# State space mixer: one 128x512 product of constants in place of two ahead of each diagonal product

## The reference, cut to what matters

```python
cum = jnp.cumsum(dtc * A.astype(f32).reshape(G, R), axis=2)
seg = jnp.exp(jnp.where(lower, cum[:, :, :, None] - cum[:, :, None, :], -jnp.inf))
cb = jnp.einsum('bnigs,bnjgs->bnijg', Cc, Bc)
y_diag = jnp.einsum('bnijg,bnijgr,bnjgrp->bnigrp', cb, seg, dtc[..., None] * xc)
```

## Time and profile before

| What | Value |
|---|---|
| Median of 3 runs | 2821.26 us (2821.2 to 2822.55) |
| The profiled execution's own time | 2822.18 us |
| Its span in the profile | 2820.0 us |
| Mean granted PE clock over the span | 0.984 |
| The mixers' stretch | about 350 to 627 us from the span's start |
| PE busy over the whole span | 2663.9 us (94%) |
| DVE, ACT and POOL busy | 1275.2, 519.9 and 585.0 us |

### The profile page before, as it was taken

The page is one execution under the profiler, slowest core; times in us unless marked ns, Lnnn a source line. Parts: engine busy times, 40 slices in busy tenths (PEclk is TensorE's granted clock), DMA queues, the critical chain, the costliest instruction groups (busy, mean ns, idle before and its releaser), DMA issues. The chain is left out here.

```text
span 2820.0 us, 45984 instructions
## 1 busy us (share of the span) xinstructions
PE 2663.9 (94%) x20286; PEld 2003.0 (71%) x20286; DVE 1275.2 (45%) x1976; ACT 519.9 (18%) x1032; POOL 585.0 (21%) x328
## 2 busy tenths in 40 slices
PE   6999889989999999999888899999999999999998
PEld 4655577764888887444676648888878754788886
DVE  1213234442899954222677544452242373544333
ACT  3222122221111101112444210000010162100001
POOL 0000055520000000001222104443334200334442
PEclk9999999999999999999999999999999999999999
DMA  6123100002222123111000011222222200222220
GB/s 288 71 109 149 60 2 2 2 28 103 80 90 90 64 82 124 45 67 54 33 3 3 3 60 60 90 90 90 90 91 90 90 1 30 89 78 79 85 90 31
DMA packets 17222, 196.33 MB, mean 70 GB/s; under 512 B 1880, under 2 KB 2008, under 8 KB 5248
## 3 DMA queue, kind: packets, MB, share of 16 engines
q1 hardware_dynamic: 17024, 193.39, 18.1%
HBM read 191.27 MB, written 2.12 MB: 69 GB/s over the span
## 5 line engine op out<-in xcount | busy, mean ns | idle before, releaser
L3217 PE MATMUL psum<-arena,weight_ring 128*128 128x256 f32 x3072 | 672.9, 381 | 2.8 <-ACT arena L3107 2.8
L3217 PEld LDWEIGHTS psum<-arena,weight_ring 128*128 128x128 f32 x3072 | 585.3, 191 | 84.9 <-ACT arena L3107 5.3
L1816 PE MATMUL psum<-arena,weight_ring 128*128 128x256 f32 x1584 | 348.2, 381 | 5.0 <-DVE arena L1992 4.0
L1816 PEld LDWEIGHTS psum<-arena,weight_ring 128*128 128x128 f32 x1584 | 302.4, 191 | 47.9 <-issue 6.4
L483 PE MATMUL psum<-arena,weight_ring 128*128 128x512 f32 (+1 forms) x672 | 248.1, 529 | 5.4 <-ACT arena L626 2.7
L2345 POOL TENSOR_TENSOR arena<-arena,consts_sb 128x512 f32<-128x512 f32 x48 | 64.6, 1353 | 902.4 <-ACT arena L2694 692.8
L483 PEld LDWEIGHTS psum<-arena,weight_ring 128*128 128x128 f32 x672 | 127.9, 193 | 117.1 <-issue 105.6
L3316 POOL TENSOR_TENSOR weight_ring<-arena,weight_ring 128x1024 f32<-128x1024 f32 x32 | 79.3, 2478 | 379.8 <-PE psum L3217 379.8
L3306 POOL TENSOR_TENSOR arena<-weight_ring 128x1024 f32<-128x1024 f32 x32 | 77.0, 2405 | 303.8 <-POOLq L3000 274.3
L226 PE MATMUL psum<-arena,weight_ring 128*128 128x512 f32 x320 | 137.8, 593 | 0.0
L3339 ACT ACTIVATE arena<-psum 128x512 f32<-128x512 f32 (+1 forms) x24 | 12.6, 524 | 622.6 <-PE psum L3217 622.6
(11 more groups left out here) (472 smaller groups left out, 3842.1 us busy)
## 6 DMA issues: line engine op xcount, KB each, us to landing
weight_ring<-in_mlp_up SPq DMA_DIRECT2D x16, 2048.0 KB, 7.8
weight_ring<-in_mlp_down SPq DMA_DIRECT2D x16, 2048.0 KB, 7.8
weight_ring<-in_ada SPq DMA_DIRECT2D x12, 2048.0 KB, 12.0
weight_ring<-in_gate_up SPq DMA_DIRECT2D x11, 2048.0 KB, 7.7
weight_ring<-in_w_in SPq DMA_DIRECT2D x7, 2048.0 KB, 10.9
weight_ring<-in_w_o SPq DMA_DIRECT2D x4, 2048.0 KB, 7.8
weight_ring<-in_w_kv SPq DMA_DIRECT2D x4, 2048.0 KB, 8.0
weight_ring<-in_down_a SPq DMA_DIRECT2D x4, 1536.0 KB, 6.5
```

The lines of the kernel that those rows point to most:

```text
L1816: mm = pe.matmul(g.banks[i][:, pair * half:(pair + 1) * half], left[:, j, pair * P:(pair + 1) * P], right(j), start=first and j == 0, stop ...
L3217: mm = pe.matmul(g.banks[i][:, pair * HALF:(pair + 1) * HALF], left[:, j, pair * P:(pair + 1) * P], right(j), start=first and j == 0, stop ...
```

## The change

One of the two products of constants ahead of each `ydiag` product is removed. Nothing else changes; all later lines of the file move up by one, so L1213 of before is L1212 of the changed kernel.

```diff
                     elif kind == "ydiag":
-                        for _ in range(2):
-                            keep_busy(pe, g, bank, SEQ)
+                        keep_busy(pe, g, bank, SEQ)
                         pe.wait_ge(s.m4, 2 * m + d + 1)
                         pe.wait_ge(s.dtx, 2 * m + d + 1)
```

## The result

| | Before | After |
|---|---|---|
| Median | 2821.23 us | 2833.94 us |
| Lowest and highest | 2818.39 to 2824.24 (6 runs) | 2826.0 to 2836.33 (6 runs) |
| Ratio to before, 95% interval | | 1.0038, 1.0022 to 1.0054 |
| Profiled execution, its span | 2822.18, 2820.0 us | 2836.33, 2834.1 us |

The change makes the kernel slower by 0.38%, some 11 us by the ratio. The forecast was 2821.4 us with a range up to 2826.0, and a chance of 0.06 for slower by over 0.2%. It forecast no change; the loss is clear of noise, and the median lies above the range.

The account below looks back on a forecast made before the run. PE was taken to bound the kernel, busy for 2663.9 of 2820.0 us. Profiled 2822.18 - 2.92 gained at d1 uses + 3.06 for two clock falls = 2822.3 us, as a median 2821.4 us; range 2817.5 to 2826.0 us.

Parts of the forecast that it names:

- the gain: At the four d1 uses PE is late, so removing a product there saves 2.92 us in sum; d0 uses gain zero.
- The 0.1 us that the forecast took back at m0 and m2: At m0 and m2 d1, the released L1213 group takes 2.00 instead of 1.90 us, reducing the gain by 0.1 us each.
- The rival in which all eight gain 6.88 us: L1440 moves up at d0 uses too, so all eight uses gain: 2814.4 us; chance 0.03.
- break even below two of them: Gain over price of a clock fall, 2.92 / 1.53 = 1.9 falls; from the second on the change doesn't pay.
- two falls, 3.06 us: Two new clock falls behind the longer PE waits at m1 and m3 d0, costing 3.06 us.
- A fall costs what the groups in it take longer: 1.53 us: Price of one clock fall in the mixers: L1109 0.82 us longer and L1205 0.71 us longer.
- six falls, 9.18 us: Upper bound of the clock term: a fall at every d0 use and two more at groups that shift, 9.18 us.
- the lengths of waits before the two falls of before: Mixer waits of 1.39 and 1.46 us preceded falls; m1 and m3 d0, at 1.57 and 2.15 us, exceed both.
- its rival on the slower side: Clock falls at all four d0 uses and once or twice elsewhere: four falls 2824.5 us, six 2827.5 us; chance 0.18.
- the program runs at PE's pace: Whole kernel: PE is busy for 2663.9 of 2820.0 us and so bounds it.

Follow-up runs that it names:

- d0_one: Kernel before with one product of constants instead of two at the four d0 uses, two kept at d1 uses; median 2829.6 us, ratio to before 1.0025.
- m3_d0_one: Kernel before with one product of constants less at m3 d0 alone; median 2823.65 us, ratio to before 1.0002.
- c_after: The changed kernel run again without any edit, as a control; ratio to before 1.0027, stretch 157.4 us.
- one_each_side: Kernel before with its two products of constants kept at each use, the second moved behind the waits for L1440 and dtx; ratio to before 1.0008.
- m1_d0_one: Kernel before with one product of constants less at m1 d0 alone; ratio to before 1.0019, profiled execution 2821.11 us.
- d1_one: Kernel before with one product of constants instead of two at the four d1 uses, two kept at d0 uses; median 2818.3 us, ratio to before 0.999.
- the kernel with three and one: Kernel before with three products of constants at d0 uses and one at d1 uses, run twice; medians 2818.02 and 2818.03 us, ratios 0.998 and 0.9992.

## Why the prediction was wrong

**Right: the gain.** The forecast gave 2.92 us at the d1 uses and nothing at the d0 uses. With the clock kept up, by the third product at d0 uses, the stretch is 3.0 us shorter in two profiles, split over the four uses as worked out (0.8, 0.9, 0.6 and 0.9 us by the steps, less 0.1 for the third product). The 0.1 us that the forecast took back at m0 and m2, for a longer group, doesn't show in the steps (0.8 and 0.6 where it had 0.71 and 0.49). The rival in which all eight gain 6.88 us has nothing for it, and the waits at d0 uses in the changed kernel (1.30, 1.72, 1.35 and 2.14 us) are close to the forecast's 1.30, 1.57, 1.35 and 2.15.

**Right: the mechanism, and that it could turn the sign.** Falls of the clock at the d0 uses were named as the place, with break even below two of them. Their number lay inside the forecast's one to three: both profiles of the changed kernel have three new ones, at m0, m1 and m3 d0, where the point took two, at m1 and m3.

**Wrong: the size of the term "two falls, 3.06 us".** The step that failed is "A fall costs what the groups in it take longer: 1.53 us". It took one fall of before, which was over after two groups, as the price of every fall. But a fall costs by how long the clock then stays down. In the earlier trace rows that was 3.4 us (from 384.72 to 388.13); behind m3 d0 it held for four groups, 10.2 us, and behind m1 d0 in one execution for 30.7 us. With the gain put back, the stretch lost 147.4 - 141.5 + 3.0 = 8.9 us in the first profile of the changed kernel, and 157.4 - 141.5 + 3.0 = 18.9 us in the second, where 3.06 were forecast. With the 0.8 us at m0 d0 ahead of the stretch that is 3.2 and 6.6 us for each of the three falls, in place of 1.53.

Measured in time at the lower level the price is steadier: 8.9 us for 21.9 us more of it, 18.9 for 45.9, in `d0_one` 7.9 for 19.6 and in `m3_d0_one` 4.4 for 10.2. That is 0.40 to 0.43 us for each microsecond, and the forecast's own 1.53 for 3.4 us is 0.45. So the price per microsecond was right and the microseconds were not. The Trainium skill (TensorE: Matmul & The Clock Gate, Terms) gives 0.5 as the penalty at half clock; the trace is somewhat below it, perhaps since PE waits for others in part of that time. Even the upper bound of the forecast (six falls, 9.18 us) was no bound: it just holds the first profile's loss, not the second's.

The unprofiled runs bear this out. Over the twelve runs of `c_after` the mean clock is 0.9799 against 0.9847, some 27 us more at the lower level in each. At 0.4 us for each that is 11 us, less 3 us gained 8 us, and the ratio of 1.0027 is 7.6 us.

**Wrong: which uses.** The forecast went by the lengths of waits before the two falls of before. `one_each_side` has waits up to 2.13 us and a mean clock of 1.00, `m1_d0_one` has one of 1.57 us and no fall, `d1_one` has a fall behind an unchanged wait of 1.29 us. The length of a wait was the wrong scale. What the two kinds of kernel differ in is the broad streaming around the wait, and the moment at which the wait comes; the changed kernel's profiles have falls at m0, m1 and m3, `d0_one` at m0, m2 and m3 (at m2 behind a wait of 1.35 us, which the changed kernel has too, without a fall). The fall that before has at 384.71 is missing in `d0_one` and `one_each_side`. The runs don't settle a rule for the moment. The forecast also counted two falls of before in the mixers where there are three: the stretch from 350 to 360 us has a mean clock of 0.83 as well. The mechanism that the prediction had as its rival on the slower side was the better guide. The Trainium skill (TensorE: Matmul & The Clock Gate, "A second HAM failure mode: psum-queue depth-cycling") describes such short idle times and repeated falls of the clock for another kernel, in bf16, and the trace agrees on the whole: 25 and 49 us at the lower level in the stretch against 3.

**Too narrow: the range.** It took the 1.35 us of three runs for the spread of the kernel. In later comparisons the kernel before alone runs from 2808 to 2833 us. PE reaches m0 d0 between 359.66 and 365.49 us in the profiles that have a product there, and 2.1 us apart in the two of the kernel with three and one, although no code ahead of it differs. A margin of that size was missing on both sides. Of the 14.1 us between the two first profiles, 5.1 are there when PE reaches the first diagonal use (365.49 against 360.43), and are of this kind: the mean clock up to 350 us is 0.96 in the first profile of the changed kernel and 0.98 in that of before. The changed kernel's own effect by ratios is 7.6 us (1.0027) to 10.7 us (1.0038).

**Not foreseen: PE's busy time grew.** The forecast started from it ("the program runs at PE's pace") but said nothing on how it would move. With sixteen passes gone it grew by 12.8 us, because products at the lower clock take longer; it doesn't measure work.

## What to carry to other kernels

A filler that hides in a wait costs nothing there, and what it buys can't be seen in its own row: price its removal by how long the clock would stay down among the products that follow, narrow ones above all, not by one fall of the trace at hand. Split an edit that touches several uses by what ends the wait at each: here the products ahead of waiting uses had to stay (a third is free), while those at uses where PE was late could go, and the kernels that do so are faster by 0.1 to 0.2%, clear of noise in two of three comparisons. Where a kernel's falls of the clock vary from execution to execution, take its spread from many runs before setting a range.

## What the runs showed of the hardware that was not expected

- PE stayed at the lower clock for 30.7 us while it was busy for 29.25 of them, mostly with products of 64 rows (`c_after`). The same groups in the kernel before, as busy, ran at a clock of 1.00: they kept the higher level where it stood and didn't bring it back where it was gone.
- The same code with the same wait of 1.29 us had no fall at 479.59 in the kernel before and one when it came at 477.24 in `d1_one`.
- A product of constants with 64 rows in place of 128 kept the clock as well here (0.99), but its 128-row neighbour and itself each took 1.05 us from start to start in place of 0.86.
- The spread of one unchanged kernel, 2808 to 2833 us, goes with its clock: 0.33 to 0.42 us for each microsecond more at the lower level.
